# An encoder trunk on one core: attention units of branch A and branch B in one mixed order, with the modulation blocks spread over 20 steps

## Chip, core and metric

One core of a Trainium2 chip runs the whole program. Its engines are named as in the profile: PE is the tensor engine (PEld its weight loads), DVE the vector engine, ACT the scalar engine, POOL the general-purpose engine, and SP issues most transfers. Each engine works through its own queue strictly in order, and they meet at semaphores. The metric is the device time of one execution in microseconds.

## What is computed

Two groups of 256 tokens (512 in all, width 1024) pass through two layers with shared weights. Cut to the part around the change:

```python
def encoder_layer(x, c, ...):
    mod = silu(c) @ w_ada + b_ada             # 6 x 1024 values: shift, scale, gate, twice
    h = rms_norm(x, norm_attn) * (1 + scale1) + shift1
    qa, ka, va, qb, kb, vb, gates = split(h @ w_in)
    # branch A: 8 heads of 64 columns, grouped keys and values, rotary positions
    ya = softmax(qa @ ka.T * scale) @ va @ w_branch_a
    # branch B: 4 heads, two maps each, a relative-position bias, then a norm per head
    p = softmax(q1 @ k1.T * scale + bias) - lam * softmax(q2 @ k2.T * scale + bias)
    yb = (rms_norm(p @ vb, subln_b) * (1 - lam_init)) @ w_branch_b
    merged = (sigmoid(g_a) * ya + sigmoid(g_b) * yb) @ w_out
    x = x + gate1 * merged
    ...                                        # mixture of 16 experts, uses shift2, scale2, gate2
```

All is float32. The two branches don't depend on each other until they are merged.

## The kernel before

A layer runs as: modulation blocks 0 to 3, input norm, projections to q, k and v, **attention**, merge (gates, branch projections), output projection, router, experts. The change is in attention, which here is work on small tiles in 28 steps.

*Units.* A unit is one head of one group of tokens, 256 queries by 256 keys. There are 16 A units (`A_UNITS`) and 8 B units (`B_UNITS`); `UNITS` lists them in the order of execution, all A first and then all B. In step i unit i is at its scores, unit i-2 at its turn, unit i-3 at its values and unit i-4, if it is a B unit, at its subln (`LAG`, `attention_steps`).

*What each engine does with a unit* (the lines are those of the kernel before, as in its profile):

- PE: scores (L886; one product for A, two for B), turn (L895: four transposes of the probabilities), values (L908) and, for B, subln (L913: sums of squares over the head).
- DVE: the maximum (L1709 for A; for B first scale and bias, L1721, then the maximum, L1728), in the next step normalising (L1737 to L1740 for A, L1742 to L1751 for B), three steps after the scores the copy of A values (L1760), five after them for B the reciprocal and product that end the subln (L1769, L1771).
- ACT: the copy of a turned unit out of PSUM (L1276), the exponentials (L1290: two for A, four for B), for B the square and the scaled copy of the values (L1308, L1309) and the square root of the subln (L1321).

Within a step DVE's order is: maximum of unit i, normalising of i-1, copy of values i-3 if that is A, end of subln of i-5 if that is B, sum of a modulation block. ACT's order is: copy of turn i-2, exponentials i, copy of a modulation block, square and scale of values i-3 if B, root of subln i-4 if B.

*Modulation blocks.* The layer's `mod` needs 12 weight blocks of 2 MB. Blocks 4 to 11 are taken in during attention, at the steps of `ADA_STEP`, every second step from step 2 to 16. In such a step PE makes the product ("rows", L749), ACT copies it (L1186), in the next step PE transposes it ("cols", L757) and in the one after DVE sums it (L1564). When the product is done, PE gives the block's slot in the ring of weight buffers back, and SP, which waits for the slots in a fixed order (`BLOCKS`), starts the next transfer into it: the last four blocks are followed by the weights of the gates and of the two branch projections.

*PSUM.* It has 8 banks, and `psum_uses` hands them out before anything runs, by turns in small rings: scores use banks 0 to 3, turns and rows share 4 and 5, and values, subln and cols share 6 and 7. A use waits (`take`) until the engine that reads the use before it in the same bank has signalled `free`: DVE for A values and cols, ACT for B values, subln, turns and rows.

```python
        elif stage in ("turn", "ada_rows"):
            yield (stage, u), (4, 5)
        else:
            yield (stage, u), (6, 7)
```

*Behind attention.* The last four steps also prepare the first weight groups of the merge (high part on ACT, L1146, low part on DVE, L1518). At step 21 ACT makes the first part of branch A's weights. The merge then runs on PE as two gate groups (24 products of 512 columns each, L718 to L720), then the first branch product, which needs DVE's four output parts (L1783), and on in turns.

Of the kernel before, what the change touches and what calls it, by code (L numbers as in the profile page):

```python
# [26 lines left out]
ACT = mybir.ActivationFunctionType  # L27
AX = mybir.AxisListType.X

P = 128  # L30
# [145 lines left out]
UNITS = A_UNITS + B_UNITS  # L176
N_UNITS = len(UNITS)

# [3 lines left out]
ADA_STEP = {2 + 2 * n: ADA_FIRST + n for n in range(ADA - ADA_FIRST)}  # L182
# [142 lines left out]
def build_trunk(nc, t_in, y_prompt, y_sample):  # L325
# [8 lines left out]
    with ctx:  # L334
# [368 lines left out]
        def _(pe):  # L703
# [103 lines left out]
            for layer in range(DEPTH):  # L807
# [60 lines left out]
                for i, stage, u in attention_steps():  # L868
# [8 lines left out]
                    if stage == "scores":  # L877
                        if u == len(A_UNITS):
                            pe.wait_ge(S["qkb_ready"], 8)
                            pe.wait_ge(S["v_ready"], 5)  # L880
# [29 lines left out]
                    else:  # L910
                        ps = take(layer_use, ("subln", u))
                        pe.wait_ge(S["ob_raw"], u - len(A_UNITS) + 1)
                        done(layer_use, ("subln", u), mm(ps[:, 0:SEQ], K("ones"), squares[:, u % 2, :],  # L913
# [163 lines left out]
        def _(act):  # L1077
# [112 lines left out]
            for layer in range(DEPTH):  # L1190
# [78 lines left out]
                for i in range(ATT_STEPS):  # L1269
# [31 lines left out]
                    if 0 <= u < N_UNITS and UNITS[u][0] == "B":  # L1301
                        _, c, _, g = UNITS[u]
                        nb = u - len(A_UNITS)
                        ps = wait_full(act, use, ("values", u))
                        if nb >= 2:

                            wait_full(act, use, ("subln", u - 2))
                        af(squares[:, u % 2, :], ps[:, 0:SEQ], ACT.Square).then_inc(S["act_own"], 1)  # L1308
                        af(qbT[:, c, g * SEQ:(g + 1) * SEQ], ps[:, 0:SEQ], ACT.Identity,  # L1309
                           scale=cur[:, PAR["subln"]:PAR["subln"] + 1]).then_inc(S["act_own"], 1)  # L1310
                        own += 2
                        act.wait_ge(S["act_own"], own)
                        nc.scalar.sem_inc(S["ob_raw"], 1)
                        nc.scalar.sem_inc(free[use[("values", u)][0]], 1)
                    u = i - LAG["subln"]
                    if 0 <= u < N_UNITS and UNITS[u][0] == "B":
                        nb = u - len(A_UNITS)
# [3 lines left out]
                        freed(af(root[:, u % 2, 0:SEQ], ps[:, 0:SEQ], ACT.Sqrt, bias=eps[:, 0:1], scale=1.0 / P),  # L1321
# [129 lines left out]
        def _(dve):  # L1451
# [154 lines left out]
            for layer in range(DEPTH):  # L1606
# [93 lines left out]
                for i in range(ATT_STEPS + 1):  # L1700
                    if i == BRANCH_STEP + 1:
                        branch_low(0)
                    if i < N_UNITS:
# [10 lines left out]
                        else:  # L1714
                            if u == len(A_UNITS):
                                dve.wait_ge(rel_back, 32)
                            for m in range(2):
                                ps = wait_full(dve, use, ("scores", u, m))
                                if m == 0:
# [36 lines left out]
                    if 0 <= u < N_UNITS and UNITS[u][0] == "A":  # L1756
# [4 lines left out]
                        dve.wait_ge(S["oa_ready"], u + 1)  # L1761
                        v.sem_inc(free[use[("values", u)][0]], 1)
                    u = i - LAG["subln"] - 1
                    if 0 <= u < N_UNITS and UNITS[u][0] == "B":
# [4 lines left out]
                        own.step(v.reciprocal(rstd[:, 0:SEQ], root[:, u % 2, 0:SEQ]))  # L1769
                        own.last()  # L1770
                        v.tensor_tensor(o, o, rstd[:, 0:SEQ], ALU.mult).then_inc(S["ob_ready"], 1)  # L1771
                        dve.wait_ge(S["ob_ready"], u - len(A_UNITS) + 1)
# [384 lines left out]
```

## Time and profile before

| | |
|---|---|
| median of 3 runs | 1762.0 us (1755.92 to 1762.78) |
| the profiled execution, its own time | 1754.14 us |
| its span, first to last instruction | 1752.1 us |
| PE busy | 1492.4 us (85%) |
| PE weight loads busy | 1108.0 us (63%) |
| DVE busy | 1063.2 us (61%) |
| ACT busy | 911.2 us (52%) |
| DVE, low part of a weight group (L1518), mean of one | 1.221 us |
| mean granted clock of PE | 0.935 |
| attention, layer 0 | about 180 to 305 us |
| attention, layer 1 | about 1023 to 1148 us |

Busy time is the time in which an engine had at least one instruction in flight. A share of the whole span says little about one stage, so the rows further down look into the stage itself: the busy times of its stretches, and the timeline, where the distance from the start of one job to the start of the next on the same engine is what the job costs there. A bracket behind a timeline row tells how long the engine was idle before it and which engine's instruction ended that. The granted clock is given as a share of 2.4 GHz; it has two levels, 1.2 and 2.4 GHz. The views give times from the start of the span; the profiled execution ran 2.0 us longer than its span.

### The profile page before, as it was taken

To read this page: it belongs to the slowest core of one execution; us is meant where nothing else is said; L and a number is where in the kernel's file an instruction comes from. 1 tells how busy PE (TensorE), PEld (TensorE's weight loads), DVE (VectorE), ACT (ScalarE), POOL (GpSimd) and SP (SyncE) were. 2 spreads that over 40 slices of the span, in tenths; PEclk is the share of its full clock that TensorE was granted. 3 is DMA by queue.
4 is the path that set the end of the run, shared out by engine and by line. 5 is a ranking of instruction groups with operands and counts; after the bars stand their busy time and mean duration, and the time that the engine had idled before them with its cause. 6 is when DMAs were issued, how large, how long until landed. Compare 5 with 4: busy or idle time off the path is not lost.

```text
span 1752.1 us, 19084 instructions
## 1 busy us (share of the span) xinstructions
PE 1492.4 (85%) x6614; PEld 1108.0 (63%) x6614; DVE 1063.2 (61%) x1369; ACT 911.2 (52%) x1196; POOL 132.8 (8%) x145
## 2 busy tenths in 40 slices
PE   3899987999948999999769999699995699999974
PEld 2577545777726777777447754478772577777763
DVE  1464479334367778778374636953356687787755
ACT  3531458223246777777263234842323577777743
POOL 1000000000000211221000000000000121112100
PEclk9899998999968999999889999899997799999997
DMA  9532660113237999889752248011132799999923
GB/s 294 189 114 78 240 193 1 49 59 130 75 131 283 350 339 338 322 324 338 279 172 96 97 163 262 8 49 48 52 141 96 262 335 335 328 349 330 325 85 144
DMA packets 163119, 341.77 MB, mean 195 GB/s; under 512 B 25062, under 2 KB 27264, under 8 KB 162928
## 3 DMA queue, kind: packets, MB, share of 16 engines
q1 hardware_dynamic: 151328, 316.68, 51.4%
q0 software_dynamic: 10992, 23.43, 3.6%
q10 hardware_dynamic: 736, 0.84, 0.2%
q8 instruction: 37, 0.61, 0.1%
q14 instruction: 26, 0.21, 0.0%
HBM read 333.58 MB, written 24.12 MB: 204 GB/s over the span
## 4 chain that ended last, share of the span: by engine, by line
PE 59%; DVE 15%; ACT 10%; issue 10%; DMA 5%; ACTq 1%; DVEq 0%; POOLq 0%; SPq 0%
PE bank L718 10%; PE bank L720 10%; PE bank L719 10%; PE bank L1016 3%; PE bank L1018 3%; PE bank L1017 3%; PE bank L749 3%; PE bank L1001 2%; PE bank L886 2%; PE bank L1002 2%; PE bank L1003 2%; DVE w_lo L2001 2%; DMA y_by_choice<-zone,row_now 2%; DMA zone<-rows_by_token,row_now 2%; PE bank L908 2%
## 5 line engine op out<-in xcount | busy, mean ns | idle before, releaser
L718 PE MATMUL bank<-x_hi,w_lo 128*128 128x512 f32 x608 | 247.4, 407 | 23.1 <-DVE x_lo L1541 13.8
L720 PE MATMUL bank<-x_hi,w_hi 128*128 128x512 f32 x608 | 240.0, 395 | 0.0
L719 PE MATMUL bank<-x_lo,w_hi 128*128 128x512 f32 x608 | 239.9, 395 | 0.0
L2001 DVE TENSOR_TENSOR w_lo<-ring,zone_r 128x2048 fp32r<-128x2048 f32 x92 | 210.4, 2291 | 27.7 <-ACT zone_r L1382 27.7
L1382 ACT CAST x_lo<-ring 128x2048 fp32r<-128x2048 f32 x96 | 183.5, 1913 | 71.9 <-PE bank L1003 34.8
L1382 ACT CAST zone_r<-ring 128x2048 fp32r<-128x2048 f32 x96 | 181.5, 1910 | 20.0 <-PE bank L1018 13.9
L1001 PE MATMUL bank<-w_lo,zone_r 128*128 128x512 f32 x384 | 161.3, 420 | 5.6 <-issue 5.6
L1518 DVE TENSOR_TENSOR w_lo<-ring,w_hi 128x1024 fp32r<-128x1024 f32 x84 | 102.6, 1221 | 85.2 <-ACT w_hi L1146 84.5
L718 PEld LDWEIGHTS bank<-x_hi,w_lo 128*128 128x128 f32 x608 | 115.5, 190 | 60.3 <-issue 22.9
L719 PEld LDWEIGHTS bank<-x_lo,w_hi 128*128 128x128 f32 x608 | 116.1, 191 | 25.6 <-issue 2.4
L720 PEld LDWEIGHTS bank<-x_hi,w_hi 128*128 128x128 f32 x608 | 116.0, 191 | 25.4
L2001 DVE TENSOR_TENSOR w_lo<-ring,x_lo 128x2048 fp32r<-128x2048 f32 x36 | 82.3, 2292 | 60.0 <-ACT x_lo L1382 60.0
L1002 PE MATMUL bank<-x_lo,zone_r 128*128 128x512 f32 x272 | 113.1, 416 | 0.0
L1003 PE MATMUL bank<-x_lo,zone_r 128*128 128x512 f32 x272 | 112.5, 413 | 0.0
L1146 ACT CAST w_hi<-ring 128x1024 fp32r<-128x1024 f32 x84 | 87.3, 1046 | 15.7 <-PE bank L720 6.1
L1003 PE MATMUL bank<-zone_r 128*128 128x512 f32 x240 | 94.3, 393 | 0.0
L1002 PE MATMUL bank<-zone_r 128*128 128x512 f32 x240 | 93.8, 391 | 0.0
L1001 PEld LDWEIGHTS bank<-w_lo,zone_r 128*128 128x128 f32 x384 | 76.0, 198 | 22.1 <-issue 6.4
L1334 ACT ACTIVATE zone<-bank 128x512 f32<-128x512 f32 x32 | 19.1, 597 | 135.6 <-PE bank L720 135.6
L2001 DVE TENSOR_TENSOR w_hi<-ring,x_lo 128x2048 fp32r<-128x2048 f32 x32 | 73.4, 2292 | 17.3 <-ACT x_lo L1382 17.1
L2089 POOL DMA_DIRECT2D rows_by_token<-zone x8 | 4.4, 549 | 936.0 <-ACT zone L1369 935.1
L2110 POOL COPY row_now<-row_i 128x1 int32 x60 | 36.1, 602 | 507.6 <-ACT zone L1419 305.5
(273 smaller groups left out, 2885.2 us busy)
## 6 DMA issues: line engine op xcount, KB each, us to landing
ring<-in_w_gate SPq DMA_DIRECT2D x32, 2048.0 KB, 13.5
ring<-in_w_up SPq DMA_DIRECT2D x32, 2048.0 KB, 14.4
ring<-in_w_down SPq DMA_DIRECT2D x32, 2048.0 KB, 8.8
ring<-in_w_ada SPq DMA_DIRECT2D x24, 2048.0 KB, 8.8
ring<-in_w_in SPq DMA_DIRECT2D x14, 2048.0 KB, 7.9
ring<-in_w_out SPq DMA_DIRECT2D x4, 2048.0 KB, 7.8
zone<-y_by_choice SPq DMA_DIRECT2D x8, 1024.0 KB, 8.0
ring<-in_w_in SPq DMA_DIRECT2D x16, 256.0 KB, 4.8
```

The costliest lines, as they stand in the source:

```text
L718: mm(out, lo, x_first, start=start, stop=False)
L719: mm(out, hi, x_second, start=False, stop=False)
L720: return mm(out, hi, x_first, start=False, stop=stop)
L749: ins = mm(ps[32 * j:32 * (j + 1), :], cs[:, k, :], w[:, k, :], start=(k < 4), stop=(k >= KC - 4))
L1001: mm(out, xg_hi[:, par, c, :], wv[:, c, :], start=(c == 0), stop=False)
L1002: mm(out, xg_lo[:, par, c, :], hi[:, k, :], start=False, stop=False)
L1003: ins = mm(out, xg_hi[:, par, c, :], hi[:, k, :], start=False, stop=(c == KC - 1))
L1016: mm(out, aT_hi[:, f, :], wv[:, f, cols], start=(f == 0), stop=False)
L1146: nc.scalar.copy(w_hi[:, n % W_BUFS, :, :], group_view(ring[SLOT[b]], b, c)).then_inc(S["w_hi_ready"], 1)
L1382: nc.scalar.copy(part_hi[buf], ring[EXPERT_SLOTS[par][k]][:, h * 2048:(h + 1) * 2048])\
L1518: v.tensor_tensor(group_view(w_lo[SLOT[b]], b, c), group_view(ring[SLOT[b]], b, c), w_hi[:, n % W_BUFS, :, :].bitcast(F32), ALU.subtract). ...
L2001: v.tensor_tensor(w_low[EXPERT_SLOTS[par][k]][:, cols], ring[EXPERT_SLOTS[par][k]][:, cols], part_hi[buf].bitcast(F32), ALU.subtract)\
```

## The change

`UNITS` becomes A, B, A eight times: B units are units 1, 4, 7 to 22. Since B units are no longer the last eight, the counts that were `u - len(A_UNITS)` become `nth_of_kind(u)`, and the waits for branch B's q, k and v (PE) and for its bias (DVE) move from unit 16 to unit 1. The modulation blocks come at steps 2, 4, 7, 9, 12, 14, 17 and 19. Nothing is computed otherwise, and no buffer changes.

```diff
-UNITS = A_UNITS + B_UNITS
+UNITS = [u for n, b in enumerate(B_UNITS) for u in (A_UNITS[2 * n], b, A_UNITS[2 * n + 1])]
 N_UNITS = len(UNITS)
+
+
+def nth_of_kind(u):
+    return sum(1 for v in UNITS[:u] if v[0] == UNITS[u][0])
+
+
+FIRST_B = UNITS.index(B_UNITS[0])
+B_AT = [UNITS.index(b) for b in B_UNITS]
...
-ADA_STEP = {2 + 2 * n: ADA_FIRST + n for n in range(ADA - ADA_FIRST)}
+ADA_STEP = {2 + 5 * n // 2: ADA_FIRST + n for n in range(ADA - ADA_FIRST)}
...
-                        if u == len(A_UNITS):
+                        if u == FIRST_B:
                             pe.wait_ge(S["qkb_ready"], 8)
                             pe.wait_ge(S["v_ready"], 5)
...
-                        pe.wait_ge(S["ob_raw"], u - len(A_UNITS) + 1)
-                        done(layer_use, ("subln", u), mm(ps[:, 0:SEQ], K("ones"), squares[:, u % 2, :],
+                        pe.wait_ge(S["ob_raw"], nth_of_kind(u) + 1)
+                        done(layer_use, ("subln", u), mm(ps[:, 0:SEQ], K("ones"), squares[:, nth_of_kind(u) % 2, :],
                                                          start=True, stop=True))
...
-                            wait_full(act, use, ("subln", u - 2))
-                        af(squares[:, u % 2, :], ps[:, 0:SEQ], ACT.Square).then_inc(S["act_own"], 1)
+                            wait_full(act, use, ("subln", B_AT[nb - 2]))
+                        af(squares[:, nb % 2, :], ps[:, 0:SEQ], ACT.Square).then_inc(S["act_own"], 1)
...
-                            if u == len(A_UNITS):
+                            if u == FIRST_B:
                                 dve.wait_ge(rel_back, 32)
                             for m in range(2):
                                 ps = wait_full(dve, use, ("scores", u, m))
-                                if m == 0:
+                                if m == 0 and u >= 3:
                                     wait_full(dve, use, ("turn", u - 3))
```

How the queues move, at the two places that matter later. In the rows the lines of the changed kernel are 8 higher than those of the kernel before from the top of the PE program on (L894 scores, L903 turn, L916 values, L921 subln, L757 rows, L765 cols, L1298 exponentials, L1329 root).

PE in layer 0, steps 5 to 7, with the PSUM banks (const, tmp, cs and zone are where operands lie). Before:

```order
L886 MATMUL bank3<-zone 128x256 x2
L895 MATMUL bank5<-const,zone 128x128 x4
L908 MATMUL bank7<-zone 64x256 x2
L757 MATMUL bank6<-const,tmp 128x128 x4
L886 MATMUL bank0<-zone 128x256 x2
L895 MATMUL bank4<-const,zone 128x128 x4
L908 MATMUL bank7<-zone 64x256 x2
L749 MATMUL bank5<-ring3,cs 32x512 x8
L886 MATMUL bank1<-zone 128x256 x2
L895 MATMUL bank4<-const,zone 128x128 x4
L908 MATMUL bank6<-zone 64x256 x2
L757 MATMUL bank7<-const,tmp 128x128 x4
```

And now, the same three steps but for the rows at the end of step 7:

```order
L894 MATMUL bank1<-zone 128x256 x2
L903 MATMUL bank5<-const,zone 128x128 x4
L916 MATMUL bank7<-zone 64x256 x2
L921 MATMUL bank6<-root,const 128x256
L765 MATMUL bank7<-const,tmp 128x128 x4
L894 MATMUL bank2<-zone 128x256 x2
L903 MATMUL bank4<-const,zone 128x128 x4
L916 MATMUL bank6<-zone 64x256 x2
L894 MATMUL bank3<-zone 128x256 x2
L894 MATMUL bank0<-zone 128x256 x2
L903 MATMUL bank5<-const,zone 128x128 x4
L916 MATMUL bank7<-zone 128x256 x2
```

Before, three uses of banks 6 and 7 come in two steps. Now step 5 alone puts values 2, subln 1 and cols 4 into banks 7, 6 and 7, and steps 6 and 7 follow with values 3 in bank 6 and values 4, those of a B unit, in bank 7.

ACT in layer 0. Before, in the first 16 units, a step with the copy of a modulation block (L1186) and one without take turns, and no table is loaded between them:

```order
L1276 COPY zone<-bank 128x512
L1290 ACTIVATE zone,psums<-bank,nmax 128x256 x2
L1186 COPY tmp<-bank 128x512
L1276 COPY zone<-bank 128x512
L1290 ACTIVATE zone,psums<-bank,nmax 128x256 x2
```

And now, from the end of step 4 to step 7:

```order
L1317 ACTIVATE zone<-bank,cur 128x256
L1284 COPY zone<-bank 128x512
L1298 ACTIVATE zone,psums<-bank,nmax 128x256 x2
L1329 ACT_TABLE_LOAD
L1329 ACTIVATE root<-bank,eps 128x256
L1284 COPY zone<-bank 128x512
L1298 ACT_TABLE_LOAD
L1298 ACTIVATE zone,psums<-bank,nmax 128x256 x2
L1284 COPY zone<-bank 128x512
L1298 ACTIVATE zone,psums<-zone,nmax 128x256 x4
```

The root of a B unit's subln now stands between exponentials, with a table load before it and another before the next exponential. Over the two layers the program before has 8 loads at the exponentials and 8 at the roots, and the changed one 14 and 14.

## Rows read from the trace of the kernel before

**Rows 1.** Busy time by stretches: us, PE, PEld, DVE, ACT, POOL, granted clock, DMA.

```profile
180.00:244.00 64.00, 60.47 (x355) 30.97 (x355) 35.45 (x108) 31.34 (x95) 0.00 (x0) 1.00 0.78 257
244.00:265.00 21.00, 14.99 (x70) 9.42 (x68) 18.26 (x47) 12.22 (x41) 0.00 (x0) 0.77 0.37 120
...
180.00:305.00 125.00, 105.60 (x543) 61.22 (x543) 91.65 (x217) 78.04 (x204) 0.00 (x0) 0.92 0.46 152
```

**Rows 2.** Timeline, PE in attention of layer 0: start, duration, what.

```profile
180.24 1.59 PEld L886 LDWEIGHTS bank<-zone 64*128 64x128 f32 x12 [0.65 <-issue]
...
200.86 1.92 PE L749 MATMUL bank<-ring,cs 128*32 128x512 f32 x16
...
202.92 1.12 PE L886 MATMUL bank<-zone 64*128 64x256 f32 x4
...
203.97 0.66 PE L895 MATMUL bank<-const,zone 128*128 128x128 f32 x4
...
204.56 1.08 PE L908 MATMUL bank<-zone 128*64 128x256 f32 x4
...
205.57 0.66 PE L757 MATMUL bank<-const,tmp 128*128 128x128 f32 x4
...
267.75 1.14 PE L886 MATMUL bank<-zone 64*128 64x256 f32 x8
...
290.37 0.59 PE L913 MATMUL bank<-root,const 128*128 128x256 f32 x2
```

**Rows 3.** Timeline, DVE and ACT with an A unit, and a block's sum.

```profile
204.08 0.69 DVE L1709 TENSOR_REDUCE nmax<-bank 128x2 f32<-128x512 f32 x1 [2.19 <-PE bank L886]
...
204.88 0.16 DVE L1737 RECIPROCAL inv<-psums 128x2 f32<-128x2 f32 x1
...
205.37 0.47 ACT L1290 ACTIVATE zone<-bank,nmax 128x256 f32<-128x256 f32 x1
...
205.84 0.42 DVE L1760 COPY zone<-bank 64x256 f32<-64x256 f32 x1
...
254.25 0.19 DVE L1564 TENSOR_REDUCE mod<-bank 128x8 f32<-128x32 f32 x1
```

**Rows 4.** Timeline, DVE through one step with B units.

```profile
272.82 1.28 DVE L1721 SCALAR_TENSOR_TENSOR zone<-bank,bias 128x512 f32<-128x512 f32 x2
...
275.39 0.17 DVE L1742 RECIPROCAL inv<-psums 128x4 f32<-128x4 f32 x1
...
277.40 1.75 DVE L1769 RECIPROCAL rstd<-root 128x256 f32<-128x256 f32 x1
...
279.65 1.29 DVE L1721 SCALAR_TENSOR_TENSOR zone<-bank,bias 128x512 f32<-128x512 f32 x2
```

**Rows 5.** Timeline, ACT through one step with B units.

```profile
280.56 0.58 ACT L1276 COPY zone<-bank 128x512 f32<-128x512 f32 x1
...
281.25 1.28 ACT L1290 ACT_TABLE_LOAD   x1
...
282.54 0.51 ACT L1290 ACTIVATE zone<-zone,nmax 128x256 f32<-128x256 f32 x1
...
284.52 0.36 ACT L1308 ACTIVATE root<-bank 128x256 f32<-128x256 f32 x1
...
285.48 1.28 ACT L1321 ACT_TABLE_LOAD   x1 [0.23 <-ACT zone L1309]
...
286.77 0.47 ACT L1321 ACTIVATE root<-bank,eps 128x256 f32<-128x256 f32 x1
```

**Rows 6.** Timeline, the end of the stage on PE and DVE.

```profile
294.54 0.58 PE L718 MATMUL bank<-x_hi,w_lo 128*128 128x512 f32 x1
...
304.88 3.10 DVE L1783 TENSOR_TENSOR zone_r<-zone,zone_r 128x512 fp32r<-128x512 f32 x5
...
307.43 0.50 PE L718 MATMUL bank<-zone_r,w_lo 128*128 128x512 f32 x1 [1.61 <-DVE zone_r L1783]
```

**Rows 7.** DMA issues from 180 to 320 us: count, KB, median us to landing.

```profile
ring<-in_w_branch_a SPq DMA_DIRECT2D x2, 1024.0 KB, 10.2
```

More of the change, by code:

```diff
@@ L1302, in _ @@
                         _, c, _, g = UNITS[u]
-                        nb = u - len(A_UNITS)
+                        nb = nth_of_kind(u)
                         ps = wait_full(act, use, ("values", u))
                         if nb >= 2:
-                            wait_full(act, use, ("subln", u - 2))
-                        af(squares[:, u % 2, :], ps[:, 0:SEQ], ACT.Square).then_inc(S["act_own"], 1)
+                            wait_full(act, use, ("subln", B_AT[nb - 2]))
+                        af(squares[:, nb % 2, :], ps[:, 0:SEQ], ACT.Square).then_inc(S["act_own"], 1)
                         af(qbT[:, c, g * SEQ:(g + 1) * SEQ], ps[:, 0:SEQ], ACT.Identity,
@@ L1316, in _ @@
                     if 0 <= u < N_UNITS and UNITS[u][0] == "B":
-                        nb = u - len(A_UNITS)
+                        nb = nth_of_kind(u)
                         ps = wait_full(act, use, ("subln", u))
@@ L1320, in _ @@
                             act.wait_ge(S["ob_ready"], nb - 1)
-                        freed(af(root[:, u % 2, 0:SEQ], ps[:, 0:SEQ], ACT.Sqrt, bias=eps[:, 0:1], scale=1.0 / P),
+                        freed(af(root[:, nb % 2, 0:SEQ], ps[:, 0:SEQ], ACT.Sqrt, bias=eps[:, 0:1], scale=1.0 / P),
                               use, ("subln", u))
@@ L1760, in _ @@
                         v.tensor_copy(qaT[rows, c, g * SEQ:(g + 1) * SEQ], ps[rows, 0:SEQ]).then_inc(S["oa_ready"], 1)
-                        dve.wait_ge(S["oa_ready"], u + 1)
+                        dve.wait_ge(S["oa_ready"], nth_of_kind(u) + 1)
                         v.sem_inc(free[use[("values", u)][0]], 1)
@@ L1768, in _ @@
                         o = qbT[:, c, g * SEQ:(g + 1) * SEQ]
-                        own.step(v.reciprocal(rstd[:, 0:SEQ], root[:, u % 2, 0:SEQ]))
+                        own.step(v.reciprocal(rstd[:, 0:SEQ], root[:, nth_of_kind(u) % 2, 0:SEQ]))
                         own.last()
                         v.tensor_tensor(o, o, rstd[:, 0:SEQ], ALU.mult).then_inc(S["ob_ready"], 1)
-                        dve.wait_ge(S["ob_ready"], u - len(A_UNITS) + 1)
+                        dve.wait_ge(S["ob_ready"], nth_of_kind(u) + 1)
                     if i - 2 in ADA_STEP:
```

## The prediction

> **What bounds the kernel now.** The change touches only the attention stage of each of the two layers, so I first asked the view by stretches where that stage lies in layer 0 and how its two halves differ [rows 1]. In the A half (180 to 244 us) PE is busy for 60.5 of 64 us and DVE for 35.5; in the B half PE falls to 15.0 of 21 us while DVE reaches 18.3. One half hangs on PE and the other on DVE, which is what a mixture could even out. The timeline then gives the length of every job, from the start of one to the start of the next on its engine.
>
> PE [rows 2]: scores of an A unit 1.05 us (202.92 to 203.97), a turn 0.6, values 1.0, the transposes of a modulation block ("cols") 0.6, the product of one ("rows") 2.05 (200.86 to 202.92). The two maps of a B unit overlap: its scores take 1.1 as well. A subln product takes 0.6. So an A unit costs PE 2.65, a B unit 3.25, a modulation block 2.65.
>
> DVE, A unit [rows 3]: maximum 0.8, normalising 0.95, copy of the values 0.4 to 0.6; a block's sum 0.2 (0.5 with the hand-offs around it). DVE, B unit [rows 4]: bias and maximum 2.6 (272.82 to 275.39), normalising 2.0, the work after subln 2.2, together 6.8: in that place DVE works without a pause.
>
> ACT [rows 3, 5]: copy of a turn 0.6 to 0.7, exponentials 1.05 for A (two of 0.47 and the read of a sum) and 2.0 for B (282.54 to 284.52), square and scale of a B value 0.95, square root 0.4. Before a square root that follows an exponential, and before the next exponential, a table load of 1.28 stands. The load before the exponential doesn't wait for the maximum: it starts right behind the copy (281.25) and is over when the exponential can begin (282.54).
>
> The stage's ends [rows 2, 6]: first scores at 180.24, first gate matmul of the merge at 294.54, first branch matmul at 307.43, which waits for DVE's low parts of the outputs (from 304.88). I count from 180.24: the gates start at 114.3, the branch at 127.2. Two gate groups fill 10.9 us on PE between (the last product's end runs on for 0.4), then PE stands 1.6 us. That 127.2 is what the change must shorten; behind it PE is again the bound.
>
> **The change, part by part.** *Bare work is unchanged.* PE: 16 x 2.65 + 8 x 3.25 + 8 x 2.65 = 89.6 us of the 114.3 before the gates. DVE: 16 x 2.3 + 8 x 6.8 + 8 x 0.5 + 4 low parts of 1.2 + 1.3 for the rest = 101.3 of the 124.6 before its output parts. The gain can only come out of 23 to 25 us of waiting per layer.
>
> *Queues in the new order.* I laid the four queues side by side with the durations above. Steps 5 to 8 serve as the example (times from the first scores; block 4's rows are done at 16.2). PE: scores 5, turn 3, values 2, subln 1 until 19.65. Then come cols 4, and they need a PSUM bank of the pair 6, 7, which values, subln and cols take by turns. It is freed by DVE's copy of values 2, and that stands behind the normalising of B unit 4, whose exponentials end at 17.3 and which runs from 18.05 to 20.1: cols 4 run from 20.6 to 21.2. Step 6 (2.65) ends at 23.85. In step 7 scores and turn end at 25.5, but values 4 need the bank of cols 4, freed by DVE's sum, and that now stands behind maximum 6, normalising 5, copy 3 and the 2.2 us after subln 1: 27.3. Values 4 and the rows of block 7 then end at 30.4. Three steps took 14.2 us, 11.2 of them work and 3.0 waits for banks.
>
> The same walk gives these starts of PE's steps: 8 at 30.4, 11 at 43.6, 14 at 58.5, 17 at 72.9, 20 at 88.8, 23 at 101.8. Its commonest waits: values 3k+2 for ACT's square and scale of the B unit just before, which stand behind 2.0 us of exponentials (1.5 us in steps 11 and 14); subln for the bank of cols (1.4); turns for DVE's normalising (2.2 in step 17, 2.4 in step 23). The last subln product ends at 114.7, so the gates start at 114.7 against 114.3: no gain there. DVE is done earlier, its output parts start at 122.1 (before: 124.6) and end at 124.6; PE's two gate groups end at 125.6, and the branch starts there without a pause instead of at 127.2. **Minus 1.6 us per layer, minus 3.2 in all.**
>
> *Table loads.* A square root now follows exponentials at seven of eight B units and six times an exponential follows it: 13 loads per layer for 7, so 6 x 1.28 = 7.7 us more on ACT. They are inside the walk: the exponential's load runs while DVE makes the maximum; the root's load stands before PE gets a bank back, and there the spare is thin: at five of the seven (units 1, 4, 10, 13, 16) the root ends only 0 to 0.6 us before PE asks. What covers them is PE's own lateness; if ACT came 1 us later, most of it would show.
> The Trainium skill, in "ScalarE: Activation LUTs", section "What ACT_TABLE_LOAD costs", gives 1283 ns for the load and 1380 ns of drain on top, 2.66 us per switch. The load agrees with the rows here; the drain doesn't show, since the root starts 1.29 us after its load does [rows 5]. By that page of the skill the addition would be 16 us per layer instead of 7.7.
>
> *Modulation blocks.* They come every 2.5 steps, the last at step 19 instead of 16. A weight transfer that waits for a freed ring slot starts later; branch A's weights follow the block of step 17 (80.9) and are needed by ACT at step 21 (96.2). They take 10.2 us to land [rows 7], until 91.1: nothing. Branch B's follow at 88.8 and are wanted only in the merge: nothing. The B units' extra waits at the front (q, k, v of branch B complete, bias back) cost at worst some tenths: ACT and DVE make those copies ahead of their first exponential and maximum anyway. DVE's first B maximum delays turn 0 from 4.1 to 5.5: in the walk.
>
> *Clock.* In the B half the granted clock is 0.77, over the whole stage 0.92 [rows 1]: part of the time it is the lower level of 1.2 GHz, where PE's pieces take twice as long. There DVE hides it. In the mixture PE is busier (about 80% through the stage), but its waits of 1.5 to 2.4 us recur and PE's pace counts everywhere. No row shows this pattern. Between nothing and the rival below I take 1.7 us for both layers, near the lower end, since the A half at 94% busy stayed at 1.00.
>
> Sum: 1754.1 - 3.2 + 1.7 = 1752.6 for the profiled execution. That one was 7.9 us under the median of the runs, 1762.0, so the forecast is **1760.5**: no change that a measurement could tell (about 0.5%, 8.8 us, is needed).
>
> **The rivals.** *The banks don't hold it up: faster.* If copies and sums come earlier than I put them, only DVE's work counts: 101.3 + 1.2 for the first scores + 8 x 0.4 for exponentials that it must await + 3 for filling and draining = 108.7 to its output parts. The last subln product ends 7.4 us before those in the walk, so at 101.3; with the gates the branch starts at 112.2, 15 us earlier. Two layers: 1762 - 30 = 1732; half of it, 1747, is as likely. For it: each engine's bare work is far under 114. Against it: one pair of banks for three kinds of use, freed by two engines in strict order.
>
> *Table loads land on the path: slower.* If ACT reaches the root over 0.6 us later than in the walk, every added load shows: 6 x (1.28 + 0.23 of idle before it [rows 5]) = 9.1 per layer, less 1.6, twice: +15, 1777. For it: the thin spare. Against it: the six loads for exponentials stay hidden behind the maximum by 1 us or more.
> The skill's same page, section "Table sets: the hidden batching unit", asks for all exponentials first and then all roots, the opposite of this change; by its 2.66 us the two layers would lose 29 us.
>
> *The clock falls: slower.* If PE's waits bring the lower level for as long as now (0.92 over 125 us, so some 20 us at half clock per layer), 10 us of PE work are added, and PE waits elsewhere for only a fifth: +8 - 1.6, twice: +13, 1775. Against it: now the low stretches come only where PE waits for DVE half of the time.
> The Trainium skill, "TensorE: Matmul & The Clock Gate", section "A second HAM failure mode: psum-queue depth-cycling", tells of a kernel whose clock went back and forth because PE paused briefly at each change of bank. The A half here has such pauses and stayed at 1.00 [rows 1]; no row shows the longer ones of the mixture.
>
> **How the numbers follow.** Forecast 0.55, banks harmless 0.20, loads 0.13, clock 0.12. The walk has some 70 hand-offs; an error of 0.05 us in each is 3.5 us per layer, so the forecast's own range is 1753 to 1768. Reaching into both sides, 8 in 10 lie in 1743 to 1776. Faster by over 0.5% (under 1753): 0.25, that is the first rival and the forecast's lower edge. Slower (over 1771): 0.22. Within: 0.53.
>
> **What would show it.** Right: 28 table loads for exponentials and roots in attention instead of 16; PE waiting in steps with cols and in the step behind; first gate matmul 113 to 117 us after the first scores, branch at once behind the two gate groups; DVE's busy time unchanged. Wrong: DVE without pauses through the stage (the first rival), values waiting for a root (the second), or a granted clock under 0.85 over the whole stage (the third).

## The result, and the profile after

The changed kernel takes **1766.0 us** (median of 8 runs, 1763.07 to 1770.33). The kernel before, run beside it on the same chip, takes 1757.1 us (8 runs, 1754.61 to 1762.78). The ratio is 1.005, with a 95% interval of 1.0034 to 1.0065: slower by half a per cent. The time lies in the range that was given, and the ratio is right at the half per cent that the forecast took for the bound of "no change". But the interval leaves no doubt of a loss, and for the stage the forecast had the wrong sign: it had expected 1.6 us less per layer, and less than 1 us more through the clock.

| | before | after |
|---|---|---|
| profiled execution, its own time | 1754.14 us | 1764.86 us |
| its span | 1752.1 us | 1763.0 us |
| branch matmul after the first scores, layer 0 | 127.2 | 134.2 |
| the same, layer 1 | 128.0 | 133.0 |
| table loads for exponentials and roots in attention | 16 | 28 |

Both layers' stages together are 12.1 us longer (7.1 and 5.0), the span is 10.9 us longer: the loss is made in attention. The granted clock of the whole program has the same mean before and after, 0.935; what moved shows only by stretches. Here are the lines that answer to those of before. All lines of the changed kernel stand 8 higher from the top of the PE program on.

The page, busy times and the granted clock in 40 slices:

```profile
PE 1495.9 (85%) x6614; PEld 1104.2 (63%) x6614; DVE 1064.7 (60%) x1369; ACT 926.7 (53%) x1208; POOL 133.3 (8%) x145
...
PEclk9899898999968999999889999999998699999997
```

Busy time by stretches (columns as in [rows 1]): the first 125 us of the stage in layer 0, and four pieces that hold most of its low clock.

```profile
180.00:305.00 125.00, 102.22 (x505) 54.11 (x505) 86.86 (x210) 80.65 (x202) 0.00 (x0) 0.89 0.46 152
180.00:192.00 12.00, 9.11 (x40) 4.53 (x39) 7.08 (x19) 5.22 (x18) 0.00 (x0) 0.69 0.53 182
245.00:253.00 8.00, 6.42 (x22) 1.65 (x22) 2.28 (x8) 2.06 (x7) 0.00 (x0) 0.57 0.12 42
262.00:268.00 6.00, 5.58 (x26) 2.07 (x26) 3.40 (x11) 3.84 (x15) 0.00 (x0) 0.72 0.00 1
292.00:301.00 9.00, 8.24 (x26) 4.69 (x26) 6.20 (x16) 7.80 (x20) 0.00 (x0) 0.62 0.01 2
```

The first row is the warning. In the same 125 us PE has fewer matmuls behind it (505 for 543), DVE and PE are both less busy, and the granted clock is 0.89 where it was 0.92. With two levels, 0.89 over 125 us is (1 - 0.89) x 125 / 0.5 = 27.5 us at 1.2 GHz; before it was 20. The four short rows show where it now lies: at the start of the stage, around step 14, around step 17, and at the last turns and values. Before, in layer 0, it lay only in the B half, in which DVE sets the pace. In layer 1 of the kernel before there is a short low stretch at the start as well, behind a wait of 2.17 us:

```profile
1023.00:1035.00 12.00, 9.68 (x51) 5.22 (x52) 6.35 (x19) 5.85 (x19) 0.00 (x0) 0.86 0.69 233
```

Timeline, PE at the start of attention of layer 0 (against [rows 2]):

```profile
179.76 2.94 PE L894 MATMUL bank<-zone 64*128 64x256 f32 x16 [0.26 <-issue]
185.44 1.09 PE L903 MATMUL bank<-const,zone 128*128 128x128 f32 x4 [2.75 <-DVEq L1762]
186.46 3.64 PE L757 MATMUL bank<-ring,cs 128*32 128x512 f32 x16
190.24 2.07 PE L894 MATMUL bank<-zone 64*128 64x256 f32 x4
...
196.68 0.66 PE L903 MATMUL bank<-const,zone 128*128 128x128 f32 x4
197.18 1.03 PE L916 MATMUL bank<-zone 128*128 128x256 f32 x4
198.13 1.92 PE L757 MATMUL bank<-ring,cs 128*32 128x512 f32 x16
```

Turn 0 waits 2.75 us for DVE, whose first B maximum now stands ahead of what it needs. Behind that wait the turn takes 1.09 us instead of 0.66, the rows product 3.64 instead of 1.92, the scores 2.07 instead of 1.12: each 1.65 to 1.9 times its length, which is the lower level. At 198 us everything has its old length again. Step 5 starts 20.4 us after the first scores; the hand walk had it at 16.2.

Timeline, PE in steps 13 to 15, and DVE beside it:

```profile
245.62 1.63 PE L916 MATMUL bank<-zone 128*64 128x256 f32 x4 [1.35 <-ACTq L1322]
248.16 1.22 PE L921 MATMUL bank<-root,const 128*128 128x256 f32 x2 [0.92 <-DVEq L1574]
249.31 3.64 PE L757 MATMUL bank<-ring,cs 128*32 128x512 f32 x16
253.09 1.12 PE L894 MATMUL bank<-zone 64*128 64x256 f32 x4
```

```profile
247.86 0.19 DVE L1572 TENSOR_REDUCE mod<-bank 128x8 f32<-128x32 f32 x1
254.25 0.69 DVE L1717 TENSOR_REDUCE nmax<-bank 128x2 f32<-128x512 f32 x1 [6.20 <-PE bank L894]
```

The waits of the first two rows are those of the walk (values for ACT's square and scale of the B unit before: 1.5 expected, 1.35 seen; subln for the bank of cols: 1.4 expected, 0.92 seen). What the walk did not have is their length in the clock: the rows product doubles again, and DVE stands idle for 6.20 us because PE is late with the next scores.

The end of the stage on DVE and PE (against [rows 6]), and the table loads of both layers:

```profile
310.14 3.10 DVE L1791 TENSOR_TENSOR zone_r<-zone,zone_r 128x512 fp32r<-128x512 f32 x5
```

```profile
314.00 0.39 PE L726 MATMUL bank<-zone_r,w_lo 128*128 128x512 f32 x1
```

```profile
L1298 ACT ACT_TABLE_LOAD x14 | 18.0, 1283 | 1.5 <-ACT zone L1284 0.4
L1329 ACT ACT_TABLE_LOAD x14 | 18.0, 1283 | 2.0 <-ACT zone L1298 1.0 <-ACT tmp L1194 0.6
```

DVE's output parts now start 3.9 us ahead of the branch (2.6 before), and the branch no longer waits for them: it stands right behind the two gate groups, as the prediction said, but the whole is late.

The working theory after this, **C** (argued so far, not shown): the waits are those of the walk, and they cost twice, once as such and once through the clock, since long PE products now fall into the low stretches. Its rivals: **B**, only the shared pair of banks matters; **T**, the twelve added table loads cost more than the walk gave them.

### The profile page after: what moved, and what is told of

It reads as the page before. It is cut to its first block, busy times and chain, and to the rows that moved or that the text cites. A ratio compares the mean times of both kernels' runs of the same rounds, so it can differ in the third digit from the quotient of the medians.

```text
span 1763.0 us, 19094 instructions
## 1 busy us (share of the span) xinstructions
PE 1495.9 (85%) x6614; PEld 1104.2 (63%) x6614; DVE 1064.7 (60%) x1369; ACT 926.7 (53%) x1208; POOL 133.3 (8%) x145
## 4 chain that ended last, share of the span: by engine, by line
PE 56%; DVE 15%; issue 10%; ACT 10%; DMA 6%; ACTq 1%; SPq 0%; DVEq 0%; POOLq 0%; PEldq 0%; PEld 0%
PE bank L726 10%; PE bank L728 10%; PE bank L727 10%; PE bank L1024 3%; PE bank L1026 3%; PE bank L1025 3%; DMA y_by_choice<-zone,row_now 2%; DMA zone<-rows_by_token,row_now 2%; PE bank L1009 2%; PE bank L1010 2%; PE bank L1011 2%; PE bank L757 2%; DVE w_lo L2009 2%; ACT x_lo L1390 1%; PE bank L916 1%
## 5 line engine op out<-in xcount | busy, mean ns | idle before, releaser
L1390 ACT CAST zone_r<-ring 128x2048 fp32r<-128x2048 f32 x96 | 181.6, 1910 | 20.4 <-PE bank L1026 13.9
```

The lines of the kernel that those rows point to most:

```text
L1390: nc.scalar.copy(part_hi[buf], ring[EXPERT_SLOTS[par][k]][:, h * 2048:(h + 1) * 2048])\
```

## The experiments

Eleven kernels were run, each beside the kernel before on the same chip. The changed kernel itself was run only with the result; where a run is set against it or against another run, the kernel before stood beside each of them with a median of 1756.0 to 1757.1 us (beside the last, one execution at 1753.2). "Branch" is always the first branch matmul, in us after the first scores, in layers 0 and 1 (127.2 and 128.0 before, 134.2 and 133.0 after).

### The two parts alone

*Only the order of units* (blocks stay at every second step):

```diff
-ADA_STEP = {2 + 5 * n // 2: ADA_FIRST + n for n in range(ADA - ADA_FIRST)}
+ADA_STEP = {2 + 2 * n: ADA_FIRST + n for n in range(ADA - ADA_FIRST)}
```

> The mixed order alone, with the modulation blocks at steps 2, 4, ... 16 as before. Theory C (the clock: waits of PE bring the lower level, and there the long products of the modulation blocks take twice as long): the blocks still meet the low level at step 2 and somewhere behind it, so the first branch matmul comes 131 to 136 us after the first scores and the time lies within 4 us of the changed kernel's 1766. Theory T (13 table loads per layer on the path): as many loads, so 1766 too. Theory B (the pair of PSUM banks shared by values, subln and cols): blocks every second step press the pair harder, so the first 16 steps take over 3 us more per layer than in the changed kernel, in all 1770 or more.

Measured: 1769.15 us (1765.96 to 1771.78), ratio 1.0071 (1.0051 to 1.009); branch 135.0 and 133.4. The mixture alone brings all of the loss, and spreading the blocks inside it does not add to it (1766.0 with it). This is what theory C gave; theory B's 1770 lies inside the runs' range and is not excluded.

*Only the spread blocks* (units in the old order):

```diff
-ADA_STEP = {2 + 2 * n: ADA_FIRST + n for n in range(ADA - ADA_FIRST)}
+ADA_STEP = {2 + 5 * n // 2: ADA_FIRST + n for n in range(ADA - ADA_FIRST)}
```

> The blocks alone at steps 2, 4, 7, ... 19, with all A units first. In the A half PE has no idle time, and it loses two blocks of 2.65 us: 5.3 us less per layer there, while the two blocks lie in steps where DVE is the bound. Theory C: PE stays dense in the A half, the granted clock there stays 1.00, and the gain of about 5 us per layer is real: 1746 to 1750, faster than the kernel before (1757). Theories T and B say the same of the A half, since no table load and little pressure on the banks is added. If the blocks' spreading itself were what costs, the time would be over 1757.

Measured: 1766.67 us (1762.48 to 1771.67), ratio 1.0054 (1.0034 to 1.0074). A miss: 1746 to 1750 was expected. The A half does gain (step 17 starts at 59.1 us instead of 62.4 in layer 0), and the B half loses more than that (branch 131.5 and 132.2). Timeline, PE and DVE in the B half of this kernel:

```profile
263.41 1.11 PE L757 MATMUL bank<-const,tmp 128*128 128x128 f32 x4 [3.62 <-ACTq L1314]
...
273.71 1.22 PE L913 MATMUL bank<-root,const 128*128 128x256 f32 x2 [4.46 <-DVEq L1566]
```

```profile
266.56 1.29 DVE L1721 SCALAR_TENSOR_TENSOR zone<-bank,bias 128x512 f32<-128x512 f32 x2 [4.29 <-PE bank L886]
```

Cols and a subln wait 3.62 and 4.46 us for the pair of banks 6 and 7. Behind them on PE stand the next scores, and so DVE, which sets the pace there, stands idle for 4.29 us. A block among B units waits for that pair of banks in either order of units.

### The table loads

Mixed order; the root of the subln is computed as a plain scaled copy (`ACT.Identity` for `ACT.Sqrt`), so 26 of the 28 loads fall away. The kernel leaves the root out, so only its attention stages are read; they do the same number of PE products in both layers.

> The changed kernel with the square root of the subln replaced by a plain scaled copy, which leaves the root out and with it 13 of the table loads per layer (the outputs differ, and with them the routing of the experts, so only the attention stage of layer 0 is to be read). Theory T: the stage from first scores to first branch matmul shortens from 134.2 by most of 13 x 1.3 = 17 us, at least by 7. Theory C: the loads are nearly hidden; it shortens by 0 to 3 us, unless the clock's low stretches fall differently (then the clock record shows it).

Measured (one execution): branch 131.3 and 128.2, that is 2.9 and 4.7 us earlier. But 1.2 and 3.1 us of that arise before step 4 (it starts at 14.7 and 11.5 for 15.9 and 14.7), where no root stands yet: the stretch at the lower level fell differently. That leaves 1.7 and 1.6 us per layer, most of it behind step 21. Theory T, in the size it needed, falls. How much of the rest is loads and how much clock is taken up in the last experiment.

### The wait at the start, filled

Mixed order; twelve idle products of 512 columns before turn 0, into the bank that the turn has already got. Nothing reads their results; the turn overwrites them.

```diff
                         ps = take(layer_use, ("turn", u))
+                        if u == 0:
+                            for _ in range(12):
+                                mm(ps[:, :], x_hi[:, 0, 0:P], x_hi[:, 0, :], start=True, stop=True)
```

> The changed kernel with 12 idle products of 512 columns on PE (2.7 us at full clock) in front of the first turn, where PE now waits 2.75 us; they write the bank that the turn then overwrites. Theory C: PE doesn't pause there, the low stretch of 7 to 10 us at the start is gone, the product of the first block takes 2.05 instead of 3.8 us, step 4 starts at 11.5 instead of 15.9 us, and each layer gains 3 to 4.5 us: about 1758. Theories T and B: PE gets more work and nothing is freed, so 1766 or slightly more.

Measured: 1768.1 us (1760.87 to 1771.13), ratio 1.0061 (1.0037 to 1.0084): no gain in the median, where theory C had expected about 1758, so this is a miss. The six runs fall into two groups: two at 1760.9 and 1762.0 with a mean clock of 0.936 and 0.937, and four at 1767.1 to 1771.1 with 0.928 to 0.931. The trace is of the run at 1762.0, with its branch at 132.6 and 129.5; it does not show where the slower four lose. Timeline, PE at the start, and two stretches of the profiled execution:

```profile
181.11 3.02 PE L902 MATMUL bank<-x_hi 128*128 128x512 f32 x12
183.98 0.60 PE L906 MATMUL bank<-const,zone 128*128 128x128 f32 x4
184.50 1.92 PE L757 MATMUL bank<-ring,cs 128*32 128x512 f32 x16
```

```profile
180.00:200.00 20.00, 18.59 (x107) 10.69 (x105) 14.72 (x42) 13.17 (x41) 0.00 (x0) 1.00 0.78 279
226.00:240.00 14.00, 12.94 (x53) 6.26 (x51) 6.98 (x15) 6.96 (x15) 0.00 (x0) 0.64 0.13 31
```

The start is at full clock, the rows product has its 1.92 us, and the steps lie on the walk (step 5 at 16.1, for 16.2 in the walk and 20.4 without the products). But a new low stretch comes at 226 us, in steps that had been at full clock (1.00 from 226 to 240 us in the changed kernel). So mending the first wait alone does not keep the clock; whether the run of waits is the cause is tried further down.

### Own banks for cols

Cols take their turn with the scores in banks 0 to 3; values and subln keep 6 and 7 to themselves.

```diff
         elif stage in ("turn", "ada_rows"):
             yield (stage, u), (4, 5)
+        elif stage == "ada_cols":
+            yield (stage, u), (0, 1, 2, 3)
         else:
             yield (stage, u), (6, 7)
```

*In the mixed order:*

> The changed kernel with the transposes of the modulation blocks (cols) in the banks of the scores, 0 to 3, instead of the pair 6, 7. Theory B (the pair of banks): the waits for that pair, 3.0 us in steps 5 to 8, fall to under 1; the same hand walk then makes DVE the bound at some 12.8 us per three steps, and each layer gains 6 to 9 us: 1748 to 1754, faster than the changed kernel by 12 to 18. Theory C (the clock alone): the low stretches stay, and with them most of the time; gain under 4 us in all. Theory T: no change, 1766.

Measured: **1751.25 us** (12 runs, 1742.23 to 1756.62), ratio 0.9965 (0.9946 to 0.9984), branch 121.8 and 123.0. That is 15 us less than the changed kernel and a little better than the one before. PE's groups from 180 to 305 us, first in the changed kernel and then in this one; the last columns are the idle time before the group and what ended it:

```profile
L916 PE MATMUL bank<-zone 128*64 128x256 f32 (+1 forms) x96 | 29.3, 435 | 6.4 <-DVEq L1574 3.1 <-ACTq L1322 2.7 <-ACT root L1329 0.4
...
L903 PE MATMUL bank<-const,zone 128*128 128x128 f32 x96 | 17.4, 309 | 9.2 <-DVEq L1762 9.2
L921 PE MATMUL bank<-root,const 128*128 128x256 f32 x16 | 7.0, 530 | 4.0 <-DVEq L1574 2.0 <-ACTq L1322 1.9
```

```profile
L918 PE MATMUL bank<-zone 128*64 128x256 f32 (+1 forms) x96 | 27.4, 411 | 0.4 <-ACT zone L1286 0.4
L896 PE MATMUL bank<-zone 64*128 64x256 f32 x123 | 26.1, 403 | 1.9 <-DVEq L1576 0.8
...
L905 PE MATMUL bank<-const,zone 128*128 128x128 f32 x96 | 16.4, 297 | 11.9 <-DVEq L1764 11.9
```

The values' waits for banks go from 6.4 to 0.4 us; those of the turns for DVE's normalising stay and grow (9.2 to 11.9). The clock over the 125 us rises from 0.89 to 0.95, and in layer 1 from 0.91 to 0.93, with nothing done about it directly. Fewer waits are one reason that fits. Another part is how the low stretches fell: at the start, where turn 0 waits 2.75 us in both kernels, the clock from 180 to 192 us is 0.86 here and 0.69 there. How the 15 us divide into banks and clock is therefore open at this point; the runs at full clock settle it.

*With the old order and spread blocks:*

> All A units first, blocks over 20 steps, cols in banks 0 to 3. With cols in the pair 6, 7 two blocks fell into steps of B units, and there PE waited 3.6 and 4.5 us for the pair. Theory B: these waits go, the gate products start about 10 us earlier than the 118.5 to 119.7 us of that run, each layer gains 8 to 12 us, in all 1744 to 1752, faster than the kernel before. Theory C alone: the B half still has the low clock in two stretches, gain under 4 us, 1763 or more.

*With the kernel before (control):*

> The kernel before with cols in banks 0 to 3: a control. In its A half PE waits for no bank, and its last cols lie in the second B step. Both theories: within 3 us of the kernel before, 1754 to 1760.

Measured: 1759.64 us (1756.93 to 1764.24, ratio 1.002, 1.0008 to 1.0032) and 1761.34 us (1756.62 to 1767.62, ratio 1.0028, 1.0013 to 1.0044). Both are misses: the first lies between the ranges of theory B and theory C, the second over the 1754 to 1760 expected. With the spread blocks the other banks bring 7 us (1766.67 with the pair), half of what they bring in the mixture; in the kernel before they cost 4.8 (1756.54 beside it). The groups of PE's scores, for 180 to 310 us, of the first and of the second:

```profile
L888 PE MATMUL bank<-zone 64*128 64x256 f32 x125 | 30.6, 417 | 7.5 <-DVEq L1568 6.3
```

```profile
L888 PE MATMUL bank<-zone 64*128 64x256 f32 x125 | 30.6, 450 | 4.5 <-DVEq L1568 3.4
```

In a stretch of B units only, each taking two of the four banks, scores now stand behind a bank that DVE's sum of a block (L1568) gives back, and that sum is late on the busiest engine: 6.3 and 3.4 us of waiting. Mixed with A units it is 0.8 us (row L896 above). So the bank change trades waits for the pair against waits of the scores: it gains where blocks fall among B units with the pair (the mixture, the spread blocks), and loses where they hardly did (the kernel before). What decides is who frees the bank, and what stands before that on its engine.

### All waits of the mixture filled

Mixed order, banks as in the change. Idle products, fewer than fill the wait, before five turns, four values and six sublns; of the waits left unfilled none is over 1 us (the longest, for cols in step 5, is 0.96):

```diff
                         ps = take(layer_use, ("turn", u))
+                        idle_products(ps, {0: 12, 9: 3, 15: 9, 21: 9, 22: 2}.get(u, 0))
...
+                        idle_before(i, {4: 7, 8: 6, 11: 6, 19: 7}.get(u, 0))
                         ps = take(layer_use, ("values", u))
...
+                        idle_before(i, {4: 4, 7: 6, 10: 6, 13: 2, 16: 5, 19: 2}.get(u, 0))
                         ps = take(layer_use, ("subln", u))
```

> The changed kernel with idle products of 512 columns on PE in all the waits over 0.4 us that the hand walk gives (2 to 12 of them, 0.23 us each at full clock, always fewer than fill the wait). Theory C: PE doesn't pause, the granted clock of the stage stays near 1.00, the steps start as in the walk (8 at 30.4, 14 at 58.5, 20 at 88.8, gates 114.7 us), the branch comes 125 to 128 us after the first scores, and the time is 1750 to 1758. If low stretches still come, the products cost time there and the time stays at 1764 to 1772. Theories T and B: the walk's waits remain as they are, and with the clock unaffected nothing changes, 1766.

Measured: **1752.8 us** (1749.47 to 1756.39), ratio 0.9974 (0.9962 to 0.9987): 13 us less than the changed kernel, by products that compute nothing and free no bank earlier. Its stage, the first gate matmul and the branch (first scores at 178.73):

```profile
180.00:305.00 125.00, 119.03 (x629) 72.74 (x626) 95.09 (x221) 87.43 (x212) 0.00 (x0) 1.00 0.46 152
```

```profile
293.25 0.58 PE L726 MATMUL bank<-x_hi,w_lo 128*128 128x512 f32 x1
...
304.36 0.39 PE L726 MATMUL bank<-zone_r,w_lo 128*128 128x512 f32 x1
```

At a granted clock of 1.00 the steps can be laid against the walk. PE's step starts after the first scores, layer 0:

| step | 5 | 8 | 11 | 14 | 15 | 17 | 20 | 23 | gates | branch |
|---|---|---|---|---|---|---|---|---|---|---|
| walk | 16.2 | 30.4 | 43.6 | 58.5 | – | 72.9 | 88.8 | 101.8 | 114.7 | 125.6 |
| filled | 16.1 | 30.4 | 43.4 | 58.0 | 66.9 | 72.7 | 88.7 | 102.0 | 114.5 | 125.6 |
| changed | 20.4 | 34.7 | 47.7 | 62.0 | 73.3 | 79.1 | 96.3 | 109.6 | 123.3 | 134.2 |

The walk holds to within 0.5 us everywhere (it gives no start for step 15). The distance between the filled kernel and the changed one, 8.6 us in layer 0 and 7.3 in layer 1 (133.0 against 125.7), is what the clock takes.

Not all of it reaches the end of the program. In the two profiled executions the stages are 15.9 us shorter together and the span 10.3 (1763.0 to 1752.7): from the branch of layer 0 to the first scores of layer 1 it is 720.3 us for 716.7, and from the second branch to the end 602.4 for 599.3. No run shows why.

### Both mended, and the kernel before with its waits filled

*Mixed order, own banks, and idle products in the six turns and two sublns that still wait:*

```diff
+                        idle_products(ps, {0: 12, 6: 6, 9: 4, 12: 4, 15: 11, 21: 14}.get(u, 0))
...
+                        idle_before(i, {4: 4, 16: 5}.get(u, 0))
```

> Edit: the mixed order with its own banks for cols (they take turns with the scores in banks 0 to 3), and in the waits of over 0.6 us that its trace still shows on PE, idle products of 512 columns into the bank that the waiting turn has already got (12 before turn 0, 6 before turn 6, 4 before turns 9 and 12, 11 before turn 15, 14 before turn 21, 4 and 5 before two sublns). Theory C (waits cost twice, once as such and once through the clock): the order with own banks alone has 13.6 and 16.9 us at the lower level per attention stage, at its start, at turn 15 and at turn 21; without them the branch comes 3 to 5 us earlier per layer (118 to 119 us after the first scores against 121.8 and 123), so 1742 to 1748. Theory B (only the bank waits counted, the clock is worth nothing once they are gone): as without the products, 1751. Slower than 1755 would mean that the idle products themselves get in the way.

*The kernel before, with idle products in seven turns:*

```diff
+                        idle_products(ps, {0: 10, 16: 6, 17: 11, 18: 8, 20: 5, 21: 3, 22: 13}.get(u, 0))
```

> Control. Edit: the kernel before, with idle products in the waits of its own that its trace shows at turns 0, 16 to 18 and 20 to 22. Theory C as told so far (the lower clock costs in the mixture because PE's pace counts everywhere, and in the B half DVE's work hides it): at most 3 us are gained in both layers (the start of the stage, where PE counts), so 1754 to 1758 against 1757. Its rival: the kernel before pays for its 20 us at the lower level as well; then the branch comes 3 us or more earlier per layer (124 us after the first scores against 127.2 and 128) and the time is 1751 or less, and what the mixture lost against it is less a matter of the order than of filled waits.

Measured: **1739.6 us** for the first (1737.84 to 1741.89), ratio 0.9903 (0.9884 to 0.9922), branch 118.3 and 118.4; 1753.2 us for the second (1751.47 to 1756.83), ratio 0.9978 (0.9963 to 0.9993), branch 126.9 and 126.6. Both times are a little under the ranges of theory C; the branches are in its range for the first, and for the second far from the 124 of its rival. The stage of layer 0 in each:

```profile
180.00:305.00 125.00, 118.83 (x632) 74.47 (x633) 99.01 (x226) 89.38 (x215) 0.00 (x0) 1.00 0.46 152
```

```profile
180.00:305.00 125.00, 112.70 (x598) 67.66 (x597) 91.41 (x216) 77.65 (x203) 0.00 (x0) 0.99 0.46 152
```

The control decides what the 13 us of filling mean. Both orders can be brought to nearly full clock (1.00 in the mixture; 0.99 and, in layer 1, 0.97 in the old order). The old order gains 2.7 us from it, the mixture 13: in the B half of the old order DVE had hidden most of the low level, as the prediction said, and in the mixture more of it shows. But filled, the two orders stand level, 1752.8 and 1753.2 us, with the branch 1.3 and 0.9 us earlier in the mixture: as long as cols keep the pair of banks, the mixture is worth next to nothing at any clock.

Own banks at full clock, 125.6 and 125.7 to 118.3 and 118.4, bring 7.3 us per layer, and 1752.8 to 1739.6 in the medians: most of the 15 us seen without filling were the banks'. With both mended the stage is 8.8 and 9.6 us shorter than before per layer, 18.4 together, and the kernel 16.4 us faster than the one before (1755.97 beside it). It is the fastest of all that were run. The old order with spread blocks, own banks and filled waits was not run, so how much of the 16.4 us needs the mixture is open.

### The loads at full clock

The kernel with all waits filled, and the root as a plain scaled copy.

> Edit: the mixed order with filled waits (granted clock 1.00 through attention), and the root of the subln computed as a plain scaled copy, so that 26 of the 28 table loads fall away. The outputs are then not those of the reference; only the attention stage is to be read, by its branch matmul, 125.6 and 125.7 us after the first scores with the loads. Theory W (as in the prediction: at full clock the loads lie beside other work): the branch comes at most 1 us earlier, 124.6 or later, and the 2.9 and 4.7 us that the same edit gained without filling came through the clock. Theory T (the loads cost something by themselves): 2 us or more per layer, 123.6 or earlier, most of it in the last steps, where a root's load stands right before the product that ends the subln.

Measured (one execution): branch 125.0 and 124.9 for 125.6 and 125.7: 0.7 us per layer for all 13 loads, within what theory W allowed. Two limits: the idle products stayed at their length and would hide a shorter wait, and it is one execution. Steps 9 and 21, which have no product, are 0.2 and 0.5 us shorter each. The 2.9 and 4.7 us that the same edit gained at the mixture's own clock were then for the most part the clock's.

## Why the prediction was wrong

It said 1760.5 us, no change; it is 1766.0, slower by 0.5%. That 1766.0 lies inside the forecast's own range of 1753 to 1768 is luck: the range was made for errors of the walk, and the walk had hardly any.

- **Bare work unchanged.** Right: PE's products and their lengths at full clock are those of [rows 2], DVE's whole busy time is 1064.7 us for 1063.2.
- **The walk through four queues.** Right, and more closely than could be hoped: its gates at 114.7 and branch at 125.6 are met at 114.5 and 125.6 as soon as the clock stays up. Its conclusion, that the pair of banks eats the whole gain of the mixture, is right too: giving cols other banks in the mixed order brings 15 us, and 7.3 us per layer at full clock.
- **The end of the stage, minus 1.6 us per layer.** Right at full clock: 1.5 and 2.2 us (125.6 and 125.7 against 127.2 and 128.0). Against the old order with its waits filled too it is 1.3 and 0.9 us.
- **The table loads, inside the walk.** Right as far as tested: 0.7 us per layer for all 13 loads. By the 2.66 us per switch of the Trainium skill, "ScalarE: Activation LUTs", section "What ACT_TABLE_LOAD costs", an estimate for the six added loads is 16 us per layer. The load of 1283 ns agrees with every row here; the drain of 1380 ns doesn't show, since the load starts 0.23 us after the instruction before it and the root 1.29 us after its load does [rows 5].
- **The clock, plus 1.7 us for both layers.** This is the step that failed. It measured 8.6 and 7.3 us, 15.9 in all (changed kernel against the one with filled waits). The step reasoned from the A half, which stayed at 1.00 while 94% busy, to a mixture with waits of 0.7 to 2.75 us every few steps, and took a value near the lower bound because no row showed the pattern. Two things before the change could have spoken. The only place of layer 0 where such waits come again and again, the B half, was the only one at 0.77 [rows 1]. And in layer 1 the kernel before falls to the lower level at the start of its A half, behind one wait of 2.17 us (0.86 from 1023 to 1035 us); the prediction read its stretches from layer 0, where a wait of 2.18 us in that place left the clock at 1.00. Mixing the units carries that place's waits into steps where PE sets the pace, and where the long rows products stand.
- **The rival "the clock falls"** was the right one, at a chance of 0.12. Its price of 8 us per layer was right (8.6 and 7.3), but by two errors that offset each other. It took 20 us at the lower level, 10 us of PE work, and let four fifths of that show. The stages of layers 0 and 1, first scores to branch:

```profile
179.76:314.00 134.24, 111.46 (x544) 61.80 (x545) 95.65 (x222) 87.03 (x211) 0.00 (x0) 0.90 0.43 141
1030.74:1163.70 132.96, 110.08 (x544) 61.39 (x545) 95.79 (x222) 86.97 (x211) 0.00 (x0) 0.91 0.43 143
```

  That is some 27 and 24 us at the lower level, 13 and 12 us of PE's time at half clock, of which some six tenths showed. And the sign that the prediction set for this rival, a clock under 0.85 over the stage, did not come: the loss was there at 0.90. The Trainium skill, "TensorE: Matmul & The Clock Gate", section "A second HAM failure mode: psum-queue depth-cycling", which the prediction named beside it, describes this kind of loss, and here the trace agrees: 27.5 us of the first 125 at the lower level, with no wait of PE longer than 2.75 us. The rival's total for the profiled execution, 1754.1 + 2 x (8 - 1.6) = 1766.9, is 2 us from the 1764.86 measured.
- **The base.** The prediction added 7.9 us because the median of the three runs shown was 1762.0. The eight runs beside the changed kernel, which include those three, have a median of 1757.1. So 4.9 of the 7.9 us were the chance of three runs; without them the forecast would have been 1755.6 and the rival 1770.
- "The banks don't hold it up" and "table loads on the path" are both out: values wait 6.4 us for banks in layer 0, and the loads cost 0.7 us per layer.

## What to carry to other kernels

When work of an engine that waits often is mixed into work that keeps PE busy, look at where the granted clock is below 1 before the change, in every layer that the trace holds, and ask whether PE's pace decides there; after the change the same waits may lower the clock in steps that nothing hides. Lay the queues side by side by hand at full clock, then put a second price on the waits of PE: here some 25 us of waits per layer (114.7 of the walk less 89.6 of work) cost 7 to 9 us more through the clock. And before units of two kinds are mixed, see which engine frees each shared bank and what stands before that on its queue; here one line of the bank table was worth more than the order, and both together with filled waits gave 1%.

## What was not expected of the hardware

- Idle products in waits pay. They compute nothing and made the program 13 us faster in the mixture (1766.0 to 1752.8) and 2.7 us in the kernel before, by holding the granted clock at 1.00 in the one and at 0.99 and 0.97 in the other. With own banks such products brought 1751.25 to 1739.6.
- Filling one wait of several did not pay: the low stretch came elsewhere (226 us, clock 0.64), and the median did not fall (1768.1).
- Runs of one kernel differ together with their clock: with own banks the three fastest of twelve (1742.2 to 1744.6 us) have a mean of 0.939 to 0.940, the five slowest (1754.0 to 1756.6) 0.929 to 0.933. With the waits filled that kernel's six runs lie within 4.1 us instead of 14.4. For the changed kernel filling does not narrow the spread (7.3 us in eight runs, 6.9 in twelve with the products), and that the clock makes the runs differ was not tried by itself.
- In the low stretches the rows product takes 3.64 us for 1.92 and a score 2.07 for 1.12: 1.85 to 1.9 times, near the factor of two between the levels.
